# Gated memory of a two-block network: head 2's scores take the next PSUM bank but one

## The reference

```
u = x @ w_in + b_in                      # mq, mk, mv, mo, gates, and fq, fk, fv of the other half
for each head:
    w[t, s] = exp(b[t] - b[s] + i[s] - m[t])   for s <= t
    qk[t, s] = (q[t] . k[s]) * w[t, s]
    num[t] = sum_s qk[t, s] * v[s]
    den[t] = sum_s qk[t, s]
    h[t] = num[t] / max(|den[t]|, exp(-m[t]))
h_ml = sigmoid(mo) * head_norm(h)
h_fx = forgetting_attention(fq, fk, fv)        # 8 heads of width 64
y = concat(h_ml, h_fx) @ w_out
```

## Time and profile before

| | |
|---|---|
| median of 3 runs | 1244.12 us |
| the three runs | 1242.06, 1244.12, 1246.97 us |
| span of the profiled execution | 1241.6 us |
| time of the profiled execution itself | not given; it lies around the span |
| PE busy | 1195.7 us, 96% |
| POOL busy | 943.2 us, 76% |
| ACT busy | 675.2 us, 54% |
| DVE busy | 594.1 us, 48% |
| mean granted TensorE clock | 0.985 |

### The profile page before, as it was taken

One profiled execution on the slowest core, in us unless ns is written; L12 is line 12 of the kernel. 1 busy time (PEld: TensorE's weight loads), 2 busy tenths in 40 slices (PEclk: granted clock), 3 DMA queues, 4 the chain that ended last, 5 costly groups with the idle time before them and its releaser, 6 DMA issues.

```text
span 1241.6 us, 20201 instructions
## 1 busy us (share of the span) xinstructions
PE 1195.7 (96%) x7776; PEld 1068.7 (86%) x7776; DVE 594.1 (48%) x1077; ACT 675.2 (54%) x924; POOL 943.2 (76%) x746
## 2 busy tenths in 40 slices
PE   6999999999889999999989999999998998999997
PEld 6989988999878988999987777888887986888886
DVE  4754344001673354100543756777404656777712
ACT  5765565434665555443544356666537565666541
POOL 6855889898815879899695436899896874989894
PEclk9999999999999999999999899999999999999999
DMA  8843445455412545545543123565454542555451
GB/s 304 240 151 129 167 147 203 172 201 178 162 69 72 183 154 203 204 158 185 206 174 136 68 110 137 195 237 204 169 205 157 183 167 72 200 203 204 174 198 35
DMA packets 33276, 208.56 MB, mean 168 GB/s; under 512 B 3448, under 2 KB 7672, under 8 KB 8744
## 3 DMA queue, kind: packets, MB, share of 16 engines
q1 hardware_dynamic: 29728, 198.17, 44.8%
q10 hardware_dynamic: 3464, 9.19, 2.3%
HBM read 206.29 MB, written 1.59 MB: 167 GB/s over the span
## 4 chain that ended last, share of the span: by engine, by line
PE 43%; POOL 36%; issue 16%; DVE 3%; ACT 2%; DMA 0%; POOLq 0%; DVEq 0%; SPq 0%; ACTq 0%
POOL w_lo L2484 36%; PE bank L346 13%; PE bank L348 7%; PE bank L294 6%; PE bank L295 6%; PE bank L296 6%; ACT w_hi L1163 1%; PE bank L686 1%; DMA raw<-stream 0%; PE bank L409 0%; PE bank L950 0%; PE bank L680 0%; ACT arena L1608 0%; PE bank L708 0%; DVE stats L1763 0%
## 5 line engine op out<-in xcount | busy, mean ns | idle before, releaser
L2484 POOL TENSOR_TENSOR w_lo<-raw,w_hi 128x512 fp32r<-128x512 f32 x740 | 940.4, 1310 | 280.6 <-ACT w_hi L1163 280.3
L1163 ACT ACTIVATE w_hi<-raw 128x2048 fp32r<-128x2048 f32 x185 | 352.0, 1910 | 172.2 <-PE bank L296 121.9
L346 PE MATMUL bank<-xs,w_hi 128*128 128x512 f32 x1024 | 363.1, 399 | 0.7 <-DVE xs L1682 0.7
L348 PE MATMUL bank<-xs,w_lo 128*128 128x256 f32 x1024 | 288.2, 281 | 0.0
L346 PEld LDWEIGHTS bank<-xs,w_hi 128*128 128x128 f32 x1024 | 193.3, 189 | 47.9 <-DVE xs L1682 2.0
L294 PE MATMUL bank<-hT_hi,w_hi 128*128 128x256 f32 x680 | 194.7, 286 | 2.3 <-issue 1.9
L348 PEld LDWEIGHTS bank<-xs,w_lo 128*128 128x128 f32 x1024 | 194.8, 190 | 0.0
L296 PE MATMUL bank<-hT_hi,w_lo 128*128 128x256 f32 x680 | 192.4, 283 | 0.0
L294 PE MATMUL bank<-xs,w_hi 128*128 128x256 f32 x576 | 168.9, 293 | 2.5 <-issue 1.1
L295 PE MATMUL bank<-xs,w_hi 128*128 128x256 f32 x576 | 165.8, 288 | 0.0
L296 PE MATMUL bank<-xs,w_lo 128*128 128x256 f32 x576 | 165.5, 287 | 0.0
(11 more groups left out here) (333 smaller groups left out, 1564.0 us busy)
## 6 DMA issues: line engine op xcount, KB each, us to landing
raw<-stream SPq DMA_DIRECT2D x185, 1024.0 KB, 4.9
arena<-ln_rows ACTq DMA_DIRECT2D x5, 1024.0 KB, 6.7
arena<-vec_scratch ACTq DMA_DIRECT2D x8, 256.0 KB, 6.8
con<-consts SPq DMA_DIRECT2D x1, 1288.0 KB
h<-x SPq DMA_DIRECT2D x2, 512.0 KB, 7.2
out<-h SPq DMA_DIRECT2D x4, 256.0 KB, 2.3
con<-pool_mat ACTq DMA_DIRECT2D x1, 768.0 KB, 9.5
vec_scratch<-vec_row ACTq DMA_DIRECT2D x1, 512.0 KB
```

What stands on the lines that cost most here:

```text
L346: mm(o[j][:, :], hi[:, k, s], xs[:, k, :, :].rearrange("p a t -> p (a t)"), start=(k == tiles_in[0]), stop=False, skip_group_check=True)
L348: last = mm(o[j][:, 0:T], lo[:, k, s], xs_hi[:, k, :], start=False, stop=(k == tiles_in[-1]), skip_group_check=True)
L1163: af(w_hi[:, c % CUT].rearrange("p a b -> p (a b)"), raw[:, c % RAW, :], ACT.Copy)\
L2484: ins = nc.gpsimd.tensor_tensor(w_lo[:, slot_c].rearrange("p a b -> p (a b)")[:, part], raw[:, slot_r, part], w_hi[:, slot_c].rearrange("p ...
```

## The change

In `heads_between` the turn is moved on by one bank, once, ahead of head 2's scores. One bank is left out at this place.

```
@@ -965,6 +965,8 @@
             def heads_between(i):
 
                 numerators(i)
+                if i == 0:
+                    turn[0] += 1
                 scores(2 + i)
 
             dense("ev_mo", 2, between=lambda i: first_heads() if i == 0 else None, after=heads_between)
```

## The result

| | before | with the change |
|---|---|---|
| median, 22 runs each | 1246.84 us | 1240.05 us |
| lowest to highest | 1241.63 to 1250.36 | 1235.78 to 1244.65 |
| ratio (95% interval) | | 0.9946 (0.9935 to 0.9957) |
| span of the profiled execution | 1241.6 us | 1240.0 us (its own time 1241.84) |
| mean granted TensorE clock | 0.985 | 0.986 |

The change makes the kernel faster by 6.8 us between the medians, 5.4 to 8.1 us by the interval. The time forecast was 1239.7, the time measured 1240.05. But the kernel before, with 22 runs in place of 3, has a median of 1246.84 and not 1244.12. So the gain is larger than the 4.37 us of the forecast. Beside the first four experiments stand 34 runs of the kernel before, of which one took 1474 us and is left out of the ratios.

The account below looks back on a forecast made before the run. TensorE (PE), busy 96% of the 1241.6 us span, was taken as the bound. Stall -2.89 and clock -1.48 sum to -4.37 us, taking the median 1244.12 to 1239.7 us; range 1235.3 to 1243.7.

Parts of the forecast that it names:

- Rival N: Head 2's scores waited for something other than the bank, so nothing moves: 1244.1 us; chance 0.04.
- Term 1: PE's stall ahead of head 2's scores goes; they start 0.31 us after head 0's last sums: -2.89 us.
- Term 2: Clock stays at 1.00 over the 48 products of the second output-gate piece, 5.86 us in place of 7.34: -1.48 us.
- Rival B: The clock over the 48 products gives nothing back, only the stall's time is won: 1241.2 us; chance 0.17.
- Rival E: Slower: the clock falls in more Fox steps, 1245.7 us with one added long fall, 1250.1 with two; chance 0.03.
- What could be late next: Checks of bank drains, POOL's weight pieces and ACT copies with PE 4.37 us ahead; each was put at cost 0.
- The slack at head 3's decay row: Bank 1 free of head 0's output at 649.18, PE asking at 652.20: 3.02 us left, cost 0.
- Rival D: Head 3's decay row waits for head 0's output to leave bank 1, taking all the gain: 1244.1 us; chance 0.05.
- each us would be lost one for one: Price named for head 3's decay row if the 3.02 us of cover before bank 1's drain were gone.
- Further on ... cost 0: Later the chain goes through PE and the DVE and ACT work it releases; bank claims stay nearly the same: cost 0.
- rival C: The move also spares the later low clock in the Fox heads (691.84 to 702.08): -8.80 us, 1235.3; chance 0.14.
- the case that I gave 0.77: The change's measured time lies within 0.5% of the kernel before, between 1237.9 and 1250.3 us.

Follow-up runs that it names:

- the first four experiments: Old wait restored in the changed kernel, 0.9997; kernel before with PE multiplying during its stall, 0.9980, or ACT reading the gate first, 0.9968; changed kernel plus a new wait, 1.0021.
- the second set: The unaltered changed kernel run again beside the kernel before on one chip: 1240.54 us against 1247.82, ratio 0.9950 (0.9930 to 0.9969).

## Why the prediction was right, and where it was not

**The place and the mechanism: right.** The bank was what head 2's scores waited for. The drain of ACT's sigmoids left PE's waits, and putting that one wait back gave the old time to 0.0003 of it, with an interval of 0.0014 on either side. Rival N is out, and nothing is left for the other bank numbers to explain.

**Term 1, -2.89 us: right.** Scores start 0.31 us behind the sums. With the stall filled, the step is longer than with the change by just 2.89 us.

**Term 2, -1.48 us: right for the profile, too small for the runs.** In the two profiles the place differs by 4.37 us to the last digit. But I read the fall of the clock from one execution, in which it lasted 3.42 us. In the wait put back it lasted 6.8, and in four profiles with this stall L924 to L924 took 13.19, 14.48, 14.72 and 14.74 us. Less 8.82 that is 4.37 to 5.92, on the mean 5.46. So term 2 should have read 1.5 to 3.0, and 2.6 on the mean of the four. I had the spread of the three runs before me and took it for the range only. Rival B is out: the filled stall has the same wait and no fall, and is 1.0 to 4.1 us faster. Rival E did not come: no profile has a fall in the first Fox step, and with the change the second has a shorter one.

**What could be late next: right.** The slack at head 3's decay row was put at 3.02 us and is 3.00. POOL's piece came 4.36 us earlier (653.25 against 656.47 + 1.14), with 1.10 us to spare where I had 1.22. Rival D is out for the change. Its price, "each us would be lost one for one", was too low: 5.18 us of waiting cost 7.56 in the profile, the rest being clock, and 9.4 over the runs.

**"Further on ... cost 0", and rival C.** By the first feed-forward product the lead should have been 4.37 us, give or take the clock. L346 starts at 752.70 with the change and 757.69 before, which with the 1.14 makes 6.13. Of the other 1.76 us the second Fox step gave 1.66. That is rival C in part: the fall is shorter, not gone. I gave it 0.14, and held that the place of the fall in time was luck. It isn't quite: the step took 18.0 to 18.1 us in each profile with the stall and the gap unfilled, and less in each without, and the mean clock of the runs says the same of the change. How a stall reaches a fall 40 us later is open. What was not tried is the same stall at another distance. The idle ahead of the step is not all of its cause, as filling it left 14.8 or 16.3 us.

**The lead behind L346.** The prediction followed the lead no further. In the two profiles most of it is gone at the second layer norm, where PE waits before, and then with the change:

```profile
944.92 0.41 PE L409 MATMUL bank<-con,h 128*128 128x128 f32 x2 [2.30 <-DVE h L1825]
943.62 0.41 PE L409 MATMUL bank<-con,h 128*128 128x128 f32 x2 [2.30 <-DVE h L1827]
```

That is 1.30 us, and 2.44 with the 1.14, where 6.13 had been there at L346. The clock was low for 6.83 us behind the first norm in place of 3.41, which at 1.48 for 3.42 is about 1.5. The rest went in the dense feed-forward products, which ran a little slower at the same clock of 1.00: before, and then with the change,

```profile
800.00:840.00 40.00, 40.00 (x233) 35.24 (x232) 29.98 (x62) 27.62 (x38) 37.44 (x30) 1.00 0.60 215
800.00:840.00 40.00, 40.00 (x228) 34.66 (x227) 29.60 (x62) 28.58 (x38) 38.47 (x31) 1.00 0.58 212
```

It is hardly the change's doing: the kernel before taken again took 192.65 us from norm to norm and the wait put back 192.77, as the change did (192.82), against 189.13 in the first profile of before. So that profile was a lucky one in this part, as it was at the stall. Why the same products run 2% slower in one execution than in another is open.

**The sum.** 5.46 us at the place and 1.7 in the Fox step make 7.2 by the few profiles; the runs say 6.8 and 6.2 (7.3 between the medians of the second set). The time of 1239.7 was met so closely by luck, since two errors balance: the gain was 2.4 us larger than forecast, and the kernel before 2.7 us slower than its first three runs. The gain came out at 0.54%, on the other side of the 0.5% from the case that I gave 0.77, though with an interval (0.43% to 0.65%) that holds both.

**The rules.** That groups should rotate through different banks (the Trainium skill, Perfetto Trace Analysis, section Optimizing Tensor Performance) agrees with the trace, where ACT reads bank 2 at 645.67 beside PE's products, but it says nothing about which bank comes next: one left out cost nothing. The gap that the Trainium skill lets pass (TensorE: Matmul & The Clock Gate, section Why this matters for your kernels), which is longer than this one, does not hold here: in each of the four profiles in which PE idled for 2.8 us at this place the clock fell, and with PE busy in it it didn't.

## What to carry to other kernels

With a fixed turn of buffers, look at which result stood in the one that comes next, and who frees it; a buffer whose reader is late is cheap to leave out, if those that follow have been free for long. Price an idle stretch of TensorE as its length plus the low clock behind it, if there is one, and read the latter from several executions, for it was twice as long in some as in others. The same holds for the time of the kernel before: three runs put its median 2.7 us too low. Where a wait can't be taken away, products that nobody reads can hold the clock; they must end before the wait does, and the fall may come in another place.

## What the runs showed of the hardware

- After 2.8 us of idle PE the granted clock was 0.50 for 3.4 or 6.8 us in all profiles of this place, sometimes from the first product on. After 5.18 us it was 0.50 for 6.8 us. After 1.01 us it stayed at 1.00 (one profile), and so it did when PE multiplied in those 2.8 us.
- Products of 128 x 128 by 128 x 128 in full precision hold the higher level at the norms too: 0.71, 0.83 and 0.86 became 1.00. 9 of them filled 2.2 us of waiting; 14 took 3.3 us and ate the gain.
- The fall in the second Fox step stays with its gap filled: 3.4 us in three profiles and 6.8 in one. In the kernel before it is 10.2 us without the filling. There the products are thin (12 or 4 rows). They alone did not bring a fall in the first step.
- Dense products at a granted clock of 1.00 ran at slightly different rates in different executions: 233 or 228 of them in the same 40 us.
